# Three edits to a two-block transformer kernel: masks of the maxima on VectorE, turned blocks stored through SyncE's queue, last output weights loaded during the attention

## What is computed

```python
x = first_block(...)    # eight causal "forgetting" heads, eight heads with a window of 128 and a sink
return second_block(x)  # indexer picks 256 keys per query; latent attention; a recurrence beside it

# first block, forgetting head                      # first block, window head
s = q @ k.T * scale + cum[q] - cum[k]               s = q @ k.T * scale, in blocks of 128
s = where(key <= query, s, -inf)                    s = where(0 <= query - key < 128, s, -inf)
o = softmax(s) @ v                                  o = softmax([s, sink])[..., :-1] @ v
y = concat(o * silu(z)) @ w_out                     x = x + gate * rms_norm(y)

# second block
proj = h @ w_in; a = attention(top 256 keys); r = hgrn2(...)
y = concat([a * silu(gate_a), rms_norm(r) * silu(gate_h)]) @ w_out
h = layer_norm(2 ** 0.25 * h + y)
```

## Time and profile before

| what | value |
|---|---|
| time before, median of 3 runs (lowest, highest) | 3589.8 us (3586.64, 3595.63) |
| the profiled execution's own time | 3588.72 us, of which 3586.8 us is the span from first to last instruction |
| busy over the span | PE 3257.0 us (91%), DVE 2200.4 (61%), ACT 1407.9 (39%), POOL 899.7 (25%) |
| first attention | from 682.60 to 1431.50: PE 691.38 of 748.90 us, DVE 503.21 |
| turn | from 1622.90 to 1674.30: PE 20.27 of 51.40 us |
| small projection | from 1674.30 to 1748.00: PE 66.91 of 73.70 us |
| last output product | from 3378.10 to 3586.80: PE 180.21 of 208.70 us |

### The profile page before, as it was taken

One profiled execution on the slowest core, in us unless ns is written; L12 is line 12 of the kernel. 1 busy time (PEld: TensorE's weight loads), 2 busy tenths in 40 slices (PEclk: granted clock), 3 DMA queues, 4 the chain that ended last, 5 costly groups with the idle time before them and its releaser, 6 DMA issues. The chain is left out here.

```text
span 3586.8 us, 43584 instructions
## 1 busy us (share of the span) xinstructions
PE 3257.0 (91%) x15488; PEld 2483.1 (69%) x15488; DVE 2200.4 (61%) x4049; ACT 1407.9 (39%) x2383; POOL 899.7 (25%) x832
## 2 busy tenths in 40 slices
PE   4999999899999998995889999997897899999798
PEld 4799888656666665784667787886775566666486
DVE  7111011366666666432189999995774689998666
ACT  5000001134444444212157999442555233333354
POOL 0111111356455451000321333334321311211000
PEclk9999999899999999997999999998998799999899
DMA  5322223565454442446211235364233622422344
GB/s 205 106 80 76 82 88 119 138 139 131 103 125 107 102 97 93 138 132 226 72 51 45 83 106 186 99 173 145 92 118 98 176 58 65 99 61 57 122 147 132
DMA packets 331914, 400.80 MB, mean 112 GB/s; under 512 B 100324, under 2 KB 249188, under 8 KB 319124
## 3 DMA queue, kind: packets, MB, share of 16 engines
q1 hardware_dynamic: 259256, 288.60, 28.5%
q10 hardware_dynamic: 67488, 78.03, 7.1%
q0 software_dynamic: 4960, 31.46, 3.2%
HBM read 265.39 MB, written 132.62 MB: 111 GB/s over the span
## 5 line engine op out<-in xcount | busy, mean ns | idle before, releaser
L2238 PE MATMUL f_pO<-f_PT,f_vv 128*128 128x512 f32 (+3 forms) x944 | 382.0, 487 | 22.2 <-ACT f_PT L2268 22.2
L2332 DVE TENSOR_REDUCE f_mxc<-f_pM 128x1 f32<-128x512 f32 (+2 forms) x448 | 239.9, 540 | 218.1 <-PE f_pM L2167 127.4
L2268 ACT ACTIVATE f_PT<-f_pS 128x512 f32<-128x512 f32 (+3 forms) x472 | 221.3, 472 | 353.4 <-PE f_pS L2206 173.8
L2893 DVE TENSOR_SCALAR_CACHE_REDUCE sharedI<-xI,TI 128x768 bf16<-128x768 f32 (+10 forms) x276 | 339.6, 1297 | 5.5 <-DVE TI L2899 5.2
L2697 PE MATMUL cbank<-hT_high,cw_hi 128*128 128x512 f32 x800 | 318.5, 398 | 19.1 <-DVE cw_lo L2852 6.8
L583 PE MATMUL p_bank<-hT_high,p_w_hi 128*128 128x512 f32 (+1 forms) x768 | 304.5, 396 | 30.5 <-DVE p_w_lo L706 30.5
L2268 ACT ACTIVATE n_PT<-n_pS 128x512 f32<-128x512 f32 (+4 forms) x352 | 176.7, 504 | 362.1 <-PE n_pS L2218 199.0
L2697 PE MATMUL cbank<-hT_high,cw_lo 128*128 128x512 f32 x800 | 315.8, 395 | 0.0
L2697 PE MATMUL cbank<-hT_low,cw_hi 128*128 128x512 f32 x800 | 315.5, 394 | 0.0
L2238 PE MATMUL n_pO<-n_PT,n_vv 128*128 128x512 f32 (+4 forms) x704 | 308.6, 520 | 0.0
L583 PE MATMUL p_bank<-hT_low,p_w_hi 128*128 128x512 f32 (+1 forms) x768 | 303.5, 395 | 0.0
(11 more groups left out here) (423 smaller groups left out, 7305.4 us busy)
## 6 DMA issues: line engine op xcount, KB each, us to landing
f_zz<-scratch_z ACTq DMA_DIRECT2D x128, 128.0 KB, 2.9
c_w_first<-in_w_in_dram SPq DMA_DIRECT2D x26, 512.0 KB, 4.4
cw_raw<-in_w_in_dram SPq DMA_DIRECT2D x25, 512.0 KB, 4.4
p_w_raw<-in_w_in_dram SPq DMA_DIRECT2D x22, 512.0 KB, 4.2
lent<-scratch_qkb POOLq DMA_DIRECT2D x40, 256.0 KB, 10.7
scratch_z<-p_stage ACTq DMA_DIRECT2D x32, 256.0 KB, 2.4
scratch_qk_high<-p_stage ACTq DMA_DIRECT2D x32, 256.0 KB, 2.6
scratch_qk_low<-p_stage_low ACTq DMA_DIRECT2D x32, 256.0 KB, 3.2
```

The source lines that it names most:

```text
L2238: pe.matmul(pO[:, B % 2, c0:c1], lhsT=vv[0:nk, b, kt, :], rhs=PT[0:nk, u % PR, c0:c1], start=(kt == 0 and not heads[h].local), stop=(heads ...
L2268: act.activation(PT[0:nk, u % PR, c0:c1], pS[0:nk, u % SR, c0:c1], ACT.Exp, scale=0.125).then_inc(s_ex, 1)
L2332: v.tensor_reduce(to, pM[:, n % 2, 0:wd], AX.X, ALU.max).then_inc(s_mx, 1)
L2893: own_.up(v.tensor_scalar(junk_v[:, own_.at % 2, 0:(i + 1) * P], scores(i), T[:, j:j + 1], None, compare, ALU.add, accum_out=count[:, j:j ...
```

## The change

1. In the first attention the two mask products into `pM` are dropped. For the 256 masked chunks DVE uses the custom instruction that the second attention has, with `mask` (local heads) or the new `last_mask` (plain heads) as second operand and `junk` laid over `maskf`. The other 192 chunks keep the plain reduction. POOL makes `last_mask` with two more instructions at the start. The masks of `pS` stay with PE.
2. In the turn, SP instead of POOL stores blocks 2 and 3, behind its 16 loads.
3. The four pieces of `o_wraw` are loaded during the second attention instead: `chosen`, the masks of its maxima, now outlives the stage, and its first 8192 columns take the weights (`over`). SP loads them after the store of the last head's third block, when all maxima are taken. POOL loads nothing in `stage_out`.
4. In `stage_out` SP issues the first `o_gT` ahead of everything else.

```diff
@@ stage_out
-            def load_turned(n, b, r):
+            def load_turned(n, b, r, first=False):
+                if n == 0 and not first:
+                    return
...
             parts = ((3, load_parts),) if part is not None else ()
+            load_turned(0, 0, 0, first=True)
             skeleton(parts + ((2, load_turned), (-1, store), (1, load_rows)), load_vectors)
...
-        @block.gpsimd
-        def _(gp):
-            for k in range(DC - MORE, DC, 2):
-                gp.dma_start(more[:, k - (DC - MORE):k - (DC - MORE) + 2, :],
-                             w_out[0, k * P:(k + 2) * P, :].rearrange("(k p) n -> p k n", p=P)).then_inc(s_w[k // 2], 16)
@@ stage_turn
+            for b in range(2, NT // NB):
+                for j in range(NB):
+                    sp.wait_ge(s_lo[j], b + 1)
+                for part in range(2):
+                    sp.dma_start(HT[part, b - 2], blocks[part][b][:].bitcast(F32)).then_inc(stored, 16)
...
-            for b in range(2, NT // NB):
-                for j in range(NB):
-                    gp.wait_ge(s_lo[j], b + 1)
-                for part in range(2):
-                    gp.dma_start(HT[part, b - 2], blocks[part][b][:].bitcast(F32)).then_inc(stored, 16)
@@ stage_attend
+            last_mask = m.sb(n_("lastmask"), [P, QB4], BF16)
+            junk = maskf[:].rearrange("p z a b -> p (z a b)").bitcast(BF16).rearrange("p (z k) -> p z k", z=2)
...
+                if j == 2 and h == NH - 1 and late:
+                    sp.wait_ge(s_mx, len(sw.chunks))
+                    for to, src, loaded in late:
+                        sp.dma_start(to, src).then_inc(loaded, 16)
...
+                step(gp.memset(last_mask[:], 0.0))
+                step(gp.tensor_copy(last_mask[:, QB4 - P:QB4], maskf[:, 0, 1]))
...
-                if hd.local:
-                    own_mask = mask[:, 0].rearrange("p a b -> p (a b)")[:, 2 * P - wd:2 * P]
-                    last = pe.matmul(bank, lhsT=identb[:], rhs=own_mask, start=False, stop=True, skip_group_check=True)
-                elif rel is None and c == sw.parts(h, i) - 1:
-                    last = pe.matmul(pM[:, n % 2, wd - P:wd], lhsT=identb[:], rhs=mask[:, 0, 1], start=False, stop=True,
-                                     skip_group_check=True)
...
-                if rel is None:
-                    v.tensor_reduce(to, pM[:, n % 2, 0:wd], AX.X, ALU.max).then_inc(s_mx, 1)
+                if rel is not None:
+                    at = OFF[i] + i * NMETA + c * QB4
+                    seen = chosen[:, at:at + wd]
+                elif heads[h].local:
+                    seen = mask[:, 0].rearrange("p a b -> p (a b)")[:, 2 * P - wd:2 * P]
+                elif c == sw.parts(h, i) - 1:
+                    seen = last_mask[:, QB4 - wd:QB4]
                 else:
...
+                    v.tensor_reduce(to, pM[:, n % 2, 0:wd], AX.X, ALU.max).then_inc(s_mx, 1)
+                    return
+                if n >= 2:
+                    v.wait_ge(s_mx, n - 1)
+                v.tensor_tensor_reduce(junk[:, n % 2, 0:wd], pM[:, n % 2, 0:wd], seen, 1.0, 3.0 * NEG,
+                                       ALU.add, ALU.max, accum_out=to).then_inc(s_mx, 1)
@@ build_program
+        over = chosen[:, 0:DC * D].bitcast(F32).rearrange("p (k n) -> p k n", n=D)
+                     late=lent_weights(w_out_2, over, s_lent[2:4], DC // 2), rel=(MK, MKT, BV, BVT, chosen))
```

## The result

| | median | lowest to highest | runs |
|---|---|---|---|
| before | 3589.05 us | 3586.64 to 3595.63 | 4 |
| changed | 3540.58 us | 3531.29 to 3548.40 | 4 |

A forecast was written before the change was run, and what follows sets the result against it. PE was taken to bound plain heads, DVE local heads, POOL's drain the turn's hand-over, and one load the last stage's start. -8.6 - 15 - 8.3 = -31.9 gave 3558 us, range 3547 to 3573.

The forecast's parts named there:

- Term A: First attention: masks of 256 chunks moved from PE to DVE, -8.6 us, between -18 and +0.5.
- VectorE's price: Local heads of the first attention: 68 masked chunks cost DVE 0.092 us more each, 6.1 us, ends 0 and 10.
- the third rival: First attention: DVE takes back what PE gives, masks worth -1 to +2 us, time 3566 to 3569; chance 0.14.
- the 48 chunks: First attention: the other masked chunks, priced at nothing because gaps cover them; 4.4 us without cover.
- PE's gain: Plain heads of the first attention: dropped mask products save 2.1 us a head, 14.7 us in seven, ends 9.8 and 18.2.
- Term B: Hand-over from turn to small projection: stores through SP end the wait for POOL's drain, -15 us, between -12 and -15.5.
- The first rival: Hand-over from turn to small projection: the block still waits for the stores, the 15.5 us stay, 3573 us; chance 0.12.
- the second tile: Small projection: its weights queue behind SP's stores, up to 7.9 us behind them; cost 0 to 3 us, taken as 0.
- Term C: Start of the last stage: turned tile first and 2 MB of weights gone, PE starts earlier, -8.3 us, between -6 and -9.5.
- the slower case: First attention: `pM`'s bank is handed back later, PE waits; about 3622 us at 0.28 us a chunk; chance 0.03.
- the late weights: Small projection: second tile's weights wait behind the stores for all 7.9 us, split not overlapped, 3561 us; chance 0.05.

The follow-up runs named there:

- the later loads: Kernel before, but POOL issues each next local head's raw loads only after six units of the plain head ahead of it: 3560.51 us, ratio 0.9922.

## Why the prediction was wrong

**Term A, VectorE's price, failed.** "DVE's loss, where DVE is the bound" charged 68 masked chunks with 0.092 us each, the custom instruction's 681 ns and the read-out's 80 less the plain reduction's 669 (68 x 0.092 is 6.3, not the 6.1 written). Durations don't add up like this on VectorE: from start to start the pair takes 0.009 us more in the same place. Measured with both engines masking, the loss is 0.2 in the six local heads and 0.3 in the stage, and VectorE's busy time grew by 1.9 us where about 20 were forecast. The other half of the step, that VectorE is the bound of local heads, is not refuted: what failed is what was charged there. The same 0.092 stands in the third rival (24 us more load for VectorE) and in the 48 chunks, whose cover was not needed.

**Term A, PE's gain, was right in mechanism and a little small.** 14.7 us were forecast for third and fourth blocks, between 9.8 and 18.2; 17.4 came, because most of these masks are 256 wide and each is worth 0.13 us and not the 0.11 of the 128-wide one. The rest of the stage, which was to lose 6.1, gave 1.6, the 48 chunks priced at nothing among it.

**Term A left out the stop at head 3.** The six stops at second blocks stood in the trace of before, and the prediction took them to be unmoved by the edit. One of them was decided by the order of two issues 1.05 us apart, and the edit turned it round: 5.0 us. Masks 19.0 and this 5.0 make 24.0, where 25.3 was measured for the edit alone; the difference is within what the runs spread. Against the forecast's 8.6 this is 15.4 more: 2.7 from PE's price, 7.7 from the rest of the stage, where a loss had been charged, and 5.0 from the stop. That is nearly all of what the sum missed, 31.9 for 48.5.

**Term B was right.** -15 forecast, -14.5 measured alone. The first rival, by which the stage would still wait for the stores, is out. By the Trainium skill, "DMA: Bandwidth & Descriptors", section "Issuing engines are not separate DMA queues", all issuers' DMAs share 16 engines. The trace agrees for the bytes (391 GB/s on POOL's queue, 385 through SP's); the stage's end is not about bytes but about which engine's drain waits for them. The projection took 74.42 us, and between 74.3 and 75.3 in the kernels without this edit too (73.75 in the first profile of before), so the second tile cost nothing, as taken. Its weights came 20.8 us in; they did stand behind the stores, of which SP's last landed at 1642.52, and came up 4.5 us behind it, within the 7.9 taken as the worst (22.9 us into the stage). POOL's two operations then end at 1650.59, 1.6 us before PE needs them (23.5 us behind its first product at 1628.68). By the Trainium skill, same page, section "Queues, rings and completion order", each DMA engine takes a queue's descriptors in the order of its ring, and the trace agrees here: the weights, issued at 1629.09, came after the stores.

**Term C was right in size and half wrong in cause.** -8.3 forecast, -7.6 alone. The prediction let the gates land one issue later than before, and in the changed kernel their load took 4.86 us, so PE started at 9.6 and not 8.8 us after the last drain (8.6 by the prediction's count). And it gave the order of the loads a part that belongs to POOL's weights: the order by itself brought 1.6, the weights by themselves 6.9.

**The rivals.** DVE taking the masks' gain back (0.14) and the slower case by PE's exposed wait for the bank (0.03) did not come; nor did the late weights. The measured time lies 6.4 us below the range: term A's far end was 18 us (PE's gain at its upper bound, no loss on VectorE), where 24.0 came, for it held no case in which a stop vanishes.

**What stays open.** Whether VectorE is what bounds the local heads, as said above. And whether the clock falls behind a stop of some 3 us: in six profiles with the old attention it fell behind 33 of 35 stops of 2.4 to 5.9 us, with the new one behind 4, 1, 4 and 4 of 5. A stop of 3.76 us kept the clock and one of 2.38 us lost it, measured between PE's starts. It may not be chance alone: behind the stop at head 9 the clock stayed up in all four profiles with the new attention and in one of six with the old. The runs don't show what decides it.

## What to carry to other kernels

Price an instruction by how far it moves the start of the next one in the same place, not by its duration: a read-out of 0.08 us behind each masked chunk was charged in full, and the pair cost 0.01 more than what it replaced. Adding the work to the engine without taking it from the other is a cheap way to see it. Look through the trace of before for stops that hang on the order of two issuers, for a saving, or two small instructions, anywhere ahead of them can turn that order; a price list of instructions never shows it. Two small loads that everything waits for deserve a quiet DMA system: two of the gains here (31.5 us in the attention, 7 in the last stage) came from moving someone else's bulk loads to another time.

## What the runs showed of the hardware

The turn ended some 15 us later than its work because GpSimd's drain record (15.57 us long, from 1658.47 to 1674.04 in the trace of before) covers its outstanding DMAs, while SP's ended at 1625.78 with its stores in flight, the last of which landed at 1642.52 (changed kernel): the same 8 MB issued by SP let the next stage start 2.4 us after the last low part. In the first attention a gates' load of 256 KB takes 8.0 to 10.5 us beside 2 MB of POOL's loads, 11.2 to 11.7 beside 4 MB, and under 4.8 without them. And a stop is dearer than it is long: the six stops before cost 32.0 us in the second blocks (102.99 less the 71.02 with the later loads), while PE stands still in them for 20.1 us (22.4 from start to start, less the 0.4 of the matmul ahead of each). The other 11.9, 2.0 a stop, are put down to work at 1.2 GHz behind it (26.2 us of it in the trace, half of which is 13.1); the four stops of the changed kernel's first profile that kept the clock cost 9.6 us for 10.5 of standing still. VectorE's read-out of an accumulator costs next to nothing behind its instruction: 83 ns long, 0.009 us from start to start.
